# Keys of both kinds in one 128-column weight in the recurrence of a diffusion-backbone kernel, with complex products of 1024 columns

## What is computed

```python
def bidir_long_conv(u, h_fwd, h_bwd, skip):
    k = jnp.concatenate([h_fwd, jnp.zeros_like(h_fwd[:1]), h_bwd[:0:-1]], axis=0)
    y = jnp.fft.irfft(jnp.fft.rfft(u, n=2 * L, axis=1) * jnp.fft.rfft(k, n=2 * L, axis=0)[None], n=2 * L, axis=1)[:, :L]
    return y + u * skip

def rwkv7_scan(r, decay, k, v, kk, a, s0, reverse):
    def step(S, inp):
        r_t, w_t, k_t, v_t, kk_t, a_t = inp
        sa = jnp.einsum('bhvk,bhk->bhv', S, -kk_t)
        S = (S * w_t[:, :, None, :] + sa[..., None] * (kk_t * a_t)[:, :, None, :]
             + v_t[..., None] * k_t[:, :, None, :])
        return S, jnp.einsum('bhvk,bhk->bhv', S, r_t)
```

## Time and profile before

| what | value |
|---|---|
| three timed runs | 2149.6, 2153.88, 2154.44 us; median 2153.88 |
| the profiled execution | 2149.79 us, its span 2148.0 us |
| PE busy | 2023.6 us, 94% of the span |
| DVE, ACT, POOL busy | 799.1, 752.2, 919.4 us |
| TensorE's granted clock, mean | 0.973 of full speed |
| from the first `multiplied` to the first product of the next stage | about 636 to 891 us of the span |

### The profile page before, as it was taken

One profiled execution on the slowest core, in us unless ns is written; L12 is line 12 of the kernel. 1 busy time (PEld: TensorE's weight loads), 2 busy tenths in 40 slices (PEclk: granted clock), 3 DMA queues, 4 the chain that ended last, 5 costly groups with the idle time before them and its releaser, 6 DMA issues.

```text
span 2148.0 us, 32168 instructions
## 1 busy us (share of the span) xinstructions
PE 2023.6 (94%) x13777; PEld 1621.7 (76%) x13777; DVE 799.1 (37%) x1158; ACT 752.2 (35%) x1060; POOL 919.4 (43%) x423
## 2 busy tenths in 40 slices
PE   5999999989999688889999998999999989989997
PEld 2677877768864577667788776777888869979996
DVE  3332032262237654363212224522133346546113
ACT  1512222254344332562222124522122275545343
POOL 0443443435413320443344444444444454448884
PEclk9999999999999799899999999999999999999998
DMA  9564336323320334326533543463232232225551
GB/s 323 181 210 153 119 106 223 121 79 137 108 49 12 73 71 104 132 94 206 195 108 108 196 157 108 133 223 124 79 118 78 69 124 79 80 79 157 196 182 55
DMA packets 232190, 276.53 MB, mean 129 GB/s; under 512 B 46725, under 2 KB 201491, under 8 KB 231732
## 3 DMA queue, kind: packets, MB, share of 16 engines
q1 hardware_dynamic: 228730, 268.65, 38.4%
q10 hardware_dynamic: 3322, 5.86, 0.8%
HBM read 265.05 MB, written 9.44 MB: 128 GB/s over the span
## 4 chain that ended last, share of the span: by engine, by line
PE 82%; DVE 6%; ACT 4%; issue 3%; DMA 2%; SPq 2%; POOL 1%; ACTq 0%; POOLq 0%; DVEq 0%
PE psum L1247 82%; DMA arena<-in_ada_w 1%; DMA arena<-in_x 1%; DVE rs L2087 1%; ACT arena L883 1%; SPq L672 0%; ACTq L795 0%; DVE h L2066 0%; ACT w_hi L854 0%; ACT L945 0%; DMA arena<-v_kept 0%; DVE arena L2175 0%; SPq L658 0%; ACT arena L1195 0%; DVE h L2134 0%
## 5 line engine op out<-in xcount | busy, mean ns | idle before, releaser
L2565 POOL TENSOR_TENSOR w_lo<-arena,w_hi 128x1024 fp32r<-128x1024 f32 x332 | 815.1, 2461 | 1011.5 <-ACT w_hi L854 1009.3
L1247 PE MATMUL psum<-u_hi,w_hi 128*128 128x512 f32 (+1 forms) x1888 | 699.3, 370 | 38.5 <-ACT u_hi L883 15.2
L1247 PE MATMUL psum<-u_hi,w_lo 128*128 128x512 f32 (+1 forms) x1888 | 689.5, 365 | 0.0
L1247 PE MATMUL psum<-u_lo,w_hi 128*128 128x512 f32 (+1 forms) x1888 | 675.2, 363 | 0.0
L854 ACT ACTIVATE w_hi<-arena 128x1024 fp32r<-128x1024 f32 x332 | 349.1, 1058 | 728.1 <-PE psum L1247 717.6
L1247 PEld LDWEIGHTS psum<-u_hi,w_hi 128*128 128x128 f32 x1888 | 363.1, 192 | 130.9 <-issue 28.6
L1247 PEld LDWEIGHTS psum<-u_hi,w_lo 128*128 128x128 f32 x1888 | 363.4, 192 | 54.7
L1247 PEld LDWEIGHTS psum<-u_lo,w_hi 128*128 128x128 f32 x1888 | 359.3, 191 | 53.4 <-issue 0.5
L2036 DVE TENSOR_TENSOR tmp<-psum,tmp 128x512 f32<-128x512 f32 (+1 forms) x88 | 55.0, 625 | 585.0 <-ACT tmp L908 585.0
L1247 PE MATMUL psum<-hid_hi,w_hi 128*128 128x512 f32 (+1 forms) x704 | 257.4, 366 | 1.7 <-POOL w_lo L2565 1.2
L1247 PE MATMUL psum<-hid_hi,w_lo 128*128 128x512 f32 (+1 forms) x704 | 255.3, 363 | 0.0
(11 more groups left out here) (259 smaller groups left out, 1478.8 us busy)
## 6 DMA issues: line engine op xcount, KB each, us to landing
arena<-in_ada_w SPq DMA_DIRECT2D x48, 1536.0 KB, 6.9
arena<-in_ffn_wg SPq DMA_DIRECT2D x44, 1024.0 KB, 5.5
arena<-in_ffn_wu SPq DMA_DIRECT2D x44, 1024.0 KB, 8.0
arena<-in_ffn_wd SPq DMA_DIRECT2D x20, 2048.0 KB, 8.8
arena<-in_ev_w_in SPq DMA_DIRECT2D x6, 2048.0 KB, 7.8
arena<-in_od_w_in SPq DMA_DIRECT2D x6, 2048.0 KB, 8.6
arena<-in_ffn_wd SPq DMA_DIRECT2D x4, 1024.0 KB, 5.0
arena<-inverse_kept SPq DMA_DIRECT2D x32, 128.0 KB, 3.0
```

Source lines behind the costliest of these rows:

```text
L1247: return pe.matmul(dst, w, x, start=first_, stop=last, skip_group_check=True)
L2565: pool.tensor_tensor(piece_shape(split_lo(pc), src), src, piece_shape(split_hi(pc).bitcast(F32), src), ALU.subtract).then_inc(S("lo_done"), 1)
```

## The change

The function, engine by engine:

- **Weights.** The two kinds of key of a head lie side by side in `key_pairs` (a 128-column weight: first and second kind; on the upper partitions the other way round). `both_kinds` becomes 8 products of 128-column weights with 128 columns; `turn_keys` 16 products of 128-column weights with 64 columns.
- **Buffers.** `key_pairs` has two buffers for both kinds. The values have three (`sav[n % 3]`).
- **Key products.** A side-by-side layout puts a head's half at its own place, so every key product is made in two halves of 64 partitions and 512 columns: POOL has 12 operations per pair j instead of 8, and now also makes the second keys of j = 0 (before: DVE L2259).
- **Order.** `strict(1)` moves ahead of `both_kinds(0, 0)`, `strict(2)` into step 0 behind `turn_keys(2)`, `strict(3)` to the end of step 2. Two of the four bonus sums move ahead of `back_turned(1)`. ACT makes decays of keys and of reads apart and earlier. The copy `aa[0] <- a_first` (L1095) goes. SP's list is set anew. On DVE `lanes(0)` moves behind the rates; `lane_level(8)` of `lanes(1)` moves into step 0.
- **Products of spectra.** `multiplied` becomes 6 operations of 1024 columns with one wait inside.

```diff
-        bk0 = [by_tile(at) for at in (h[:, 0:1024], h[:, 1024:2048])]
-        bk1 = by_tile(h[:, 2048:3072])
+        key_pairs = [at.rearrange("p d c (i k t) -> p d c i k t", i=2, k=2)
+                     for at in (h[:, 0:2048].rearrange("p (d c x) -> p d c x", d=2, c=CT),
+                                big[:, 0:4096].rearrange("p (d c x) -> p d c x", d=2, c=CT)[:, :, :, 0:256])]
+        def both_keys(d, c, n, rows):
+            return key_pairs[n // 2 % 2][rows, d, c, half_of(d, n)].rearrange("p k t -> p (k t)")
...
         sav = [at.rearrange("p (e d c v) -> p e d c v", e=2, d=2, c=CT)
-               for at in (arena[:, 1024:2048], arena[:, 19456:20480])]
+               for at in (arena[:, 1024:2048], arena[:, 19456:20480], h[:, 2048:3072])]
...
 # load_values (SP)
-                if n >= 2:
-                    sp.wait_ge(S("o_mm"), n - 1)
+                if n >= 3:
+                    sp.wait_ge(S("o_mm"), n - 2)
+                elif n == 2:
+                    sp.wait_ge(S("slots_0"), 6)
...
 # both_kinds (PE)
-                        pe.wait_ge(S("a_done"), min(STEPS, n + 2 + n % 2) if n else 2)
-                        pe.wait_ge(S("slots_1"), 2 + 4 * j)
+                        pe.wait_ge(S("a_done"), 4 if n < 2 else 6 if n < 5 else 8)
+                        pe.wait_ge(S("slots_1"), 6 + 6 * j)
...
-                        for kind, key in enumerate((bk0[j % 2], bk1)):
-                            for e, rows in enumerate(rows_of):
-                                ins = mm(bank[factor_bank(n, d, e)][rows_of[e ^ kind], c * P:(c + 1) * P], key[rows, d, c, t],
-                                         two_kinds(rows, ar0[j % 3][:, d, c, t], ar1[j % 2][:, d, c, t]), True, True)
+                        for e, rows in enumerate(rows_of):
+                            ins = mm(bank[factor_bank(n, d, e)][:, c * P:(c + 1) * P], both_keys(d, c, n, rows),
+                                     two_kinds(rows, ar0[j % 3][:, d, c, t], ar1[j % 2][:, d, c, t]), True, True)
...
 # turn_keys (PE)
-                        for kind, key in enumerate((bk0[j % 2], bk1)):
-                            for e, (rows, b) in enumerate(zip(rows_of, (2, 3))):
-                                ins = mm(bank[b][rows_of[e ^ kind], at_pair(d, c, C)], key[rows, d, c, within(d, n)],
-                                         ident[rows, rows], True, True)
+                        for rows, b in zip(rows_of, (2, 3)):
+                            ins = mm(bank[b][:, at_pair(d, c, C)], both_keys(d, c, n, rows), ident[rows, rows], True, True)
...
 # the products of spectra (DVE)
-                    for i in range(2):
-                        re, im = bank[4 * s + i], bank[4 * s + 2 + i]
-                        ve.tensor_tensor(ft[0], re, kre, ALU.mult).then_inc(S("ve_steps"), v.step())
...
+                    ve.tensor_tensor(out_re, re, kre, ALU.mult).then_inc(S("ve_steps"), v.step())
+                    ve.tensor_tensor(ft, im, kim, ALU.mult).then_inc(S("ve_steps"), v.step())
+                    ve.tensor_tensor(out_im, re, kim, ALU.mult).then_inc(S("ve_steps"), v.step())
+                    ve.tensor_tensor(im, im, kre2, ALU.mult).then_inc(S("ve_steps"), v.step())
+                    ve.wait_ge(S("ve_steps"), v.n)
+                    ve.tensor_tensor(out_re, out_re, ft, ALU.subtract).then_inc(S("ve_steps"), v.step())
+                    ve.tensor_tensor(out_im, out_im, im, ALU.add).then_inc(S("ve_steps"), v.step())
...
 # the recurrence's slots (POOL)
+                pool.wait_ge(S("h_moves"), 144)
+                pool.wait_ge(S("bonus_k"), 4)
+                second_keys(0)
                 reads(0)
                 pool.wait_ge(S("first_slots"), 7)
                 receives(1)
-                pool.wait_ge(S("rates"), 1)
+                second_keys(1)
+                reads(1)
...
 # the step loop (DVE)
-                    if n in (1, 3):
-                        take_strict((n + 3) // 2)
+                    if n == 0:
+                        take_strict(2)
```

More of the change, by code:

```diff
@@ L314, in program @@
         yf = arena[:, 4096:8192].rearrange("p (s i c) -> p s i c", s=2, i=4)
-        ft = [arena[:, 8192 + i * 512:8704 + i * 512] for i in range(2)]
+        ft = arena[:, 8192:9216].rearrange("p (i c) -> p i c", i=2)
         w_up = arena[:, 9216:9728]
@@ L1037, in even_mixer @@
                 act.activation(chunk_decay, big[:, 0:4096].rearrange("p (x t) -> p x t", t=C)[:, :, C - 1], ACT.Exp, scale=-DECAY).then_inc(S("exped"), 1)
-                decays_of(0, 0)
-                decays_of(0, 1)
+                for part in ("keys", "read"):
+                    for d in range(2):
+                        decays_of(0, d, part)
+                for d in range(2):
+                    decays_of(1, d, "keys")
                 v_out(0)
@@ L1089, in even_mixer @@
                 keys_out(1)
-                act.wait_ge(S("zeroed"), 6)
+                act.wait_ge(S("zeroed"), 7)
                 z_out(0, 4)
+                for d in range(2):
+                    decays_of(2, d, "read")
                 z_out(0, 5)
                 act.wait_ge(S("hy_done"), 4)
-                act.wait_ge(S("first_slots"), 9)
-                act.activation(aa[0], a_first, ACT.Copy).then_inc(S("rates"), 1)
                 for n in range(STEPS):
@@ L1103, in even_mixer @@
                         z_out(n + 1, 4)
-                        if n in (0, 2):
-                            decays_of(n // 2 + 2, 0)
+                        if n in (1, 2):
+                            for d in range(2):
+                                decays_of(3, d, "keys" if n == 1 else "read")
                         z_out(n + 1, 5)
@@ L1575, in bonus_sum @@
                     mm(bank[SPARE[i]], blk[:, :], bonus[:, i * NT:(i + 1) * NT], True, True).then_inc(S("bonus_sum"), 1)
+                bonus_sum(0)
+                bonus_sum(1)
+                pe.wait_ge(S("hy_mul"), 4)
+                back_turned(1)
                 v_turn(2)
                 v_turn(3)
-                for i in range(4):
-                    bonus_sum(i)
+                bonus_sum(2)
+                bonus_sum(3)
+                strict(1)
                 def both_kinds(n, d):
@@ L1773, in even_mixer @@
                         widen(n + 1, 5)
+                    if n == 2:
+                        strict(3)
                 gates(2)
@@ L2379, in even_mixer @@
                 ve.sem_inc(S("first_slots"), 1)
+                lanes(0)
                 hyena_out(1)
```

228 lines of the change are left out of this document (129 added, 99 removed).

## The result

| | before | changed |
|---|---|---|
| median of 11 runs | 2147.81 us (2141.64 to 2154.44) | 2159.08 us (2154.47 to 2163.14) |
| ratio of changed to before | | 1.0052, 95% interval 1.0041 to 1.0062 |
| the profiled execution | 2149.79 us, span 2148.0 | 2154.47 us, span 2152.6 |
| matmuls on PE | 13777 | 13265 |
| GpSimd (POOL) busy | 919.4 us | 940.4 us |

The change makes the kernel 0.5% slower, 11.3 us by the medians, where 2144 us and faster was forecast, in a range of 2131 to 2158. The profiled execution of the changed kernel is its fastest of 11; one nearer the median follows with x0_again.

What follows compares the result with a forecast made beforehand. PE's own work was taken to bound the loop steps, waits the part before; 11.1 us early at `solve(1)` less 2.5 in steps 1 to 5 gave 8.6, so 2141.2, raised by half a spread to 2144 (range 2131 to 2158).

Steps and rivals of the forecast that it cites:

- `turn_keys`, +0.91 for each: PE's products with turned keys: 128-column weight loads set the pace, 1.84 us instead of 0.93, for each of 8.
- `both_kinds` unchanged but for the changes of tile: PE's products with both kinds of key: still 0.93 us, plus 0.16 for each of two new changes of tile.
- Products of spectra: DVE's calls before the loop: six 1024-column operations take 7.0 us, 1.2 less per call; `back_turned(0)` starts at 689.7.
- POOL's chain ends at 714.3, PE idles 5.3: Before `strict(1)`: POOL's 12 products from 698.2 end at about 714.3, so PE idles 5.3 us and returns at the lower clock.
- the rival of cheap half-partition products: POOL's products on 64 partitions cost 0.64 us, PE's idle before `strict(1)` goes, 5 us more gained, 2139; chance 0.13.
- DVE's two copies 1.3, and `both_kinds(0, 0)` starts at 717.4: Behind `strict(1)`, before the loop: DVE's copies take 1.3 us and PE starts `both_kinds(0, 0)` at 717.4.
- Step 0, 17.6, and step 1, 15.4: First two loop steps: step 0 takes 17.6 us instead of 23.3, step 1 takes 13.85 + 0.91 + 0.64.
- Step 2, "1.5 for DVE's lanes": Loop step 2: on top of the usual step, 0.95 us for `strict(3)`, 1.5 for DVE's lanes, 1.5 for `take_outputs(2)`.
- Steps 3 to 5, 47.0: Later loop steps: 13.85 + 0.91 + 0.64 us each, with 0.8 more in step 3 for outputs; 47.0 together.
- the waits only move: Rival: POOL at 1.47 us per product, low clock through step 0, DVE's lanes later by 2; 2150 to 2152; chance 0.18.
- The slower case: Rival: 64*128 tiles load one after another, `turn_keys` 3.68 us, `both_kinds` 1.84; 29 us more, 2173; chance 0.12.
- The count of instructions: Rival: `turn_keys` with half the instructions costs half or at most the same, worth 7.3 us, 2136.8; chance 0.15.

Runs made afterwards that it cites:

- x0_again: The changed kernel without an edit, run again for a second profile; 2159.21 us, 1.0053 to the kernel before.
- y2: The changed kernel with POOL held back beside `lanes` and much of the old order of `strict` and `lanes(1)` put back; 2141.7 us, 0.9966 to the kernel before.
- x1_narrow: The changed kernel with the products with keys back on 64-column weights; 2158.58 us, 1.0042 to the kernel before.
- y3: y2 with the products with keys back on 64-column weights; 2140.61 us, 0.9971 to the kernel before.

## Why the prediction was wrong, step by step

- **`turn_keys`, +0.91 for each:** right. 781.15 to 783.08 is 1.93 us for 32 matmuls on 64*128, forecast 1.84. The rule on LDWEIGHTS that the prediction cites (the Trainium skill, TensorE: Matmul & The Clock Gate, the section "LDWEIGHTS (loading the stationary operand)") agrees with the trace: 1.93/32 is 60 ns, with two tiles side by side 121 for each, and 128 rows had 115.
- **`both_kinds` unchanged but for the changes of tile:** right. 1.09 us (740.84 to 741.93), 0.93 + 0.16.
- **Products of spectra:** the first two calls take 7.0 us as forecast, the third and fourth, beside POOL, 7.8 and 7.25. DVE's rates behind the third (L2245) take 2.16 us where they took 1.53, and `back_turned(0)` starts at 691.4 (694.18 less 2.82), not at 689.7.
- **POOL's chain ends at 714.3, PE idles 5.3:** 2.4 late. The 12 products start at 699.8 instead of 698.2 and take 16.9 us (1.25 to 1.8 each) instead of 16.1, and `strict(1)` starts at 716.8, after 3.05 us of idle time, since the bonus sums before it were late too (2.21 us for ACT's L1035). A product on 64 partitions costs what one on 128 does, so the rival of cheap half-partition products is out.
- **"DVE's two copies 1.3, and `both_kinds(0, 0)` starts at 717.4":** the step that failed first. It starts at 724.2. The copies of `strict(1)` stand behind `lanes(0)`, for which the prediction has no term: at the 6.6 us of before DVE would have been through in time. Beside POOL `lanes(0)` takes 16.7 and keeps DVE until 721.8 on the profile's own clock; six more operations (1.28 and 2.47 us) stand between. 6.8 us late here, `solve(0)` is 6.3 late (742.7 for 736.4).
- **Step 0, 17.6, and step 1, 15.4:** 19.0 (745.55 to 764.55) and 14.9 (to 779.48). In step 1 PE waits 1.03 us for the lanes' way back through DRAM, which the prediction had as covered.
- **Step 2, "1.5 for DVE's lanes":** the same error again and the larger one. The step takes 30.3 us (779.48 to 809.75), forecast 19.35 (15.4, and 3.95 added). The part of `lanes(2)` ahead of the copy of the state stretches over 14 us (778.7 to 792.7; before 6.3), since POOL makes its products for j = 3 beside it in one go, where in the kernel before it waited 8.43 us for ACT's decays before them (at 788.80), and PE waits 7.6 us, losing its clock (0.64).
- **Steps 3 to 5, 47.0:** 44.2, 2.8 less. The loop is shorter here than the sum has it, and no run splits this by its causes.

The sum: 6.3 + 1.4 - 0.5 + 10.9 - 2.8 = 15.3 us late at `solve(6)`. That the median misses 2144 by 15.1 is chance. The forecast stands on 2149.8 and half a spread, some 2152 for the kernel before, whose median of 11 is 2147.81; set against that median the change was to gain 8.6 and loses 11.3, 19.9 apart. And this trace is of the fastest execution, which regains 3.3 us between `solve(6)` and the next stage, where the prediction had nothing change. x0_again, at the median, has `solve(6)` at 857.6, less 3.04 (its operation of DVE stands at 630.74) 854.6: 18.8 later than forecast, with the slow clock in `back_turned(0)` on top.

The waits for the single buffer and for values went as forecast. y2, in which the contention is held off, comes out at 2141.7, 5.9 us under before where 8.6 was forecast; but it has much of the old order back, so it does not confirm the terms for the order, and no run here shows a gain from the new place of `strict(1)`. What was missing is one term: the time of DVE's `lanes` was taken from rows in which POOL was idle, for a schedule in which POOL works beside them. The prediction had this contention on POOL's side (1.47 us for a product beside a busy DVE instead of 1.27), but not on DVE's. The trace of before had the sign, at 778 us:

```profile
778.16 1.02 DVE L2360 COPY h<-h 128x8 f32<-128x8 f32 x1
779.21 1.19 DVE L2349 TENSOR_TENSOR h<-h 128x8 f32<-128x8 f32 x1
780.43 0.17 DVE L2351 TENSOR_TENSOR h<-h 128x8 f32<-128x8 f32 x1
```

The first two lie beside POOL's L2636, the third does not.

Of the rivals, "the waits only move" came nearest in kind (PE waits for DVE instead of POOL), but not in size: it had 2 us for DVE's lanes. The slower case was given 0.14, 0.12 of it on a wrong mechanism, 64*128 tiles that load one after another; at 60 ns each they load side by side. The count of instructions does not rule `turn_keys`, yet it matters elsewhere, in the gaps of PE's supply.

## What to carry to other kernels

When a change frees an engine from a wait, ask which engine it will slow down while it runs: here a POOL that waited less made 8-column operations on DVE seven times as long and their chain 2.5 times, and two lines that hold it were worth 24 us in the order of y2. Read each operation's row twice, with the neighbour idle and with it busy, and take the one that fits the new schedule. Look also for waits that kept two engines apart by accident, as DVE's order did at `lanes(0)`. A change that loses may hold a gain: find the wait that is new, and move it before the rest is undone.

## What was not expected of the hardware

- An operation of DVE on 8 columns takes 0.17 us alone and up to 1.2 beside a stream of POOL's products; one of 128x64 0.25 and about 1.2; one of 128x512 1.02 and 1.7. The stretch of about 0.7 to 1.0 us hardly depends on the operation's own length, so the smallest suffer most in proportion.
- POOL's product of 512 columns takes 1.26 us on 64 partitions as on 128.
- Half as many, twice as wide matmuls cost, as an estimate, some 9 us more of PE's time over the recurrence (8 x 0.84 for `turn_keys`, 16 x 0.16 for `both_kinds`) and go with 5 to 10 us less of gaps between instructions (1.7 in x0_again for 6.8 in x1_narrow, 3.2 for 12.9, 3.4 for 8.6). What makes the gaps is not shown.
- y2's runs spread from 2136.6 to 2150.6, more than y3's (2136.4 to 2145.1); why stays open.
